# 68 late slots instead of 64, the second half's x in PSUM, and the low-part products last in each chunk

## What is computed

```python
def peer(x, w_query, sub_keys_1, sub_keys_2, expert_down, expert_up):
    ...                       # product keys: eidx [T, 128] expert numbers, g [T, 128] softmax weights
    def chunk(args):
        xi, ei, gi = args
        u = expert_down[ei]
        a = jax.nn.gelu(jnp.einsum('cd,ced->ce', xi, u)).astype(jnp.float32)
        w = (a * gi).astype(xi.dtype)
        return jnp.einsum('ce,ced->cd', w, expert_up[ei])
    ...
x = x + peer(rms_norm(x, norm_ffn_gain[l]), ...)
return rms_norm(x, norm_final_gain)
```

## Time and profile before

| | us |
|---|---|
| median of 3 runs | 2063.03 (2059.24 to 2063.68) |
| the profiled execution | 2062.69 |
| its span in the trace | 2060.8 |
| TensorE busy | 1896.1 (92% of the span) |
| VectorE busy | 1538.8 (75%) |
| ScalarE busy | 846.6 (41%) |
| POOL busy | 798.5 (39%) |
| data moved | 620.14 MB, mean 301 GB/s |

### The profile page before, as it was taken

The page is one execution under the profiler, slowest core; times in us unless marked ns, Lnnn a source line. Parts: engine busy times, 40 slices in busy tenths (PEclk is TensorE's granted clock), DMA queues, the critical chain, the costliest instruction groups (busy, mean ns, idle before and its releaser), DMA issues.

```text
span 2060.8 us, 28583 instructions
## 1 busy us (share of the span) xinstructions
PE 1896.1 (92%) x11587; PEld 1671.0 (81%) x11587; DVE 1538.8 (75%) x1856; ACT 846.6 (41%) x1108; POOL 798.5 (39%) x494
## 2 busy tenths in 40 slices
PE   8999999999999999788987466699999999999997
PEld 7989987999998789678887355578888888888876
DVE  5444446444465469899999999866888888999998
ACT  4333336333333443223322488344344444433433
POOL 1310300000000022755665788023454444777873
PEclk9999999999999999899999688799999999999999
DMA  7864540555566535999999999568999999999996
GB/s 253 294 212 164 168 139 22 165 182 183 184 224 229 191 133 210 398 426 420 425 421 413 362 427 427 212 228 326 384 407 399 392 385 383 378 408 400 395 397 268
DMA packets 142669, 620.14 MB, mean 301 GB/s; under 512 B 9680, under 2 KB 20192, under 8 KB 84464
## 3 DMA queue, kind: packets, MB, share of 16 engines
q0 software_dynamic: 46352, 336.11, 40.0%
q1 hardware_dynamic: 93712, 280.05, 37.5%
q10 hardware_dynamic: 2512, 2.75, 0.4%
HBM read 616.77 MB, written 2.10 MB: 300 GB/s over the span
## 4 chain that ended last, share of the span: by engine, by line
PE 72%; DVE 12%; POOL 7%; issue 5%; DMA 3%; ACT 1%; DVEq 0%; SPq 0%; ACTq 0%; POOLq 0%
PE psum L638 70%; POOL down_rows L1209 6%; DVE down_rows L2090 4%; DMA down_rows<-in_peer_expert_down_dram,eidx 2%; DVE w_lo L1748 1%; POOL pe_rows L1209 1%; ACT w_hi L1307 0%; PE psum L656 0%; DMA x_in<-in_x_dram 0%; DVE u_lo L2197 0%; DVE xres L2210 0%; DVE onehot L2050 0%; DVE onehot L2053 0%; DVE key L2055 0%; PE psum L981 0%
## 5 line engine op out<-in xcount | busy, mean ns | idle before, releaser
L1748 DVE TENSOR_TENSOR w_lo<-raw,w_hi 128x2048 fp32r<-128x2048 f32 x124 | 291.4, 2350 | 349.3 <-ACT w_hi L1307 349.2
L1307 ACT CAST w_hi<-raw 128x2048 fp32r<-128x2048 f32 x124 | 236.1, 1904 | 415.6 <-PE psum L638 415.6
L638 PE MATMUL psum<-u_hi,c_hi 128*128 128x512 f32 x1024 | 401.4, 392 | 3.9 <-POOL c_lo L1243 3.5
L638 PE MATMUL psum<-u_lo,c_hi 128*128 128x512 f32 x1024 | 399.4, 390 | 0.0
L638 PE MATMUL psum<-u_hi,c_lo 128*128 128x512 f32 x1024 | 399.4, 390 | 0.0
L2197 DVE TENSOR_TENSOR u_lo<-u_raw,u_hi 128x2048 fp32r<-128x2048 f32 x128 | 308.1, 2407 | 90.2 <-ACT u_hi L1657 89.0
L2090 DVE CUSTOM_DVE_ANT_0 down_rows<-down_rows,xn 128x2048 f32<-128x2048 f32 x157 | 354.1, 2286 | 6.2 <-DMA down_rows<-in_peer_expert_down_dram,eidx 4.6
L1209 POOL DMA_INDIRECT down_rows<-in_peer_expert_down_dram,eidx x157 | 271.8, 1732 | 129.2 <-issue 45.3
L638 PE MATMUL psum<-act_hi,w_hi 128*128 128x256 f32 x1088 | 310.5, 285 | 4.4 <-DVE w_lo L1748 4.4
L638 PE MATMUL psum<-act_hi,w_lo 128*128 128x256 f32 x1088 | 308.9, 284 | 0.0
L638 PE MATMUL psum<-act_lo,w_hi 128*128 128x256 f32 x1088 | 308.9, 284 | 0.0
(11 more groups left out here) (312 smaller groups left out, 3109.0 us busy)
## 6 DMA issues: line engine op xcount, KB each, us to landing
u_raw<-in_peer_expert_up_dram SPq DMA_DIRECT2D x128, 1024.0 KB, 6.6
raw<-in_w_in_dram SPq DMA_DIRECT2D x76, 1024.0 KB, 5.0
raw<-in_w_out_dram SPq DMA_DIRECT2D x16, 1024.0 KB, 5.0
raw<-in_peer_w_query_dram SPq DMA_DIRECT2D x16, 1024.0 KB, 5.0
raw<-in_w_up_nsa_dram SPq DMA_DIRECT2D x8, 1024.0 KB, 4.9
raw<-in_w_up_fox_dram SPq DMA_DIRECT2D x8, 1024.0 KB, 4.9
cmp_w<-in_k_cmp_w_dram SPq DMA_DIRECT2D x4, 1024.0 KB, 10.7
cmp_w<-in_v_cmp_w_dram SPq DMA_DIRECT2D x4, 1024.0 KB, 10.6
```

The source lines that it names most:

```text
L638: return nc.tensor.matmul(*a, skip_group_check=True, **k)
L1307: nc.scalar.copy(w_hi[:, p % 2], raw[:, p]).then_inc(hi_done, 1)
L1748: tt(w_lo[:, p % 2], raw[:, p], f32(w_hi[:, p % 2]), ALU.subtract).then_inc(lo_done, 1)
```

## The change

Four slots of the second half move from the gather stage to the late slots (`DENSE` 60, `LATE` 68), and the loops over slots run to `NT` = 188. The second half's x is put into banks 0 to 3 by four matmuls with the identity, as is already done for the first half (at `XRES_AT`), so `xres[:, 1]` is free from the first chunk on and serves as a sixth late buffer; the additions go to a tile of its own, `late_sum`, from step 67 on. In `up_chunk` the eight products with `u_lo` come last, behind a wait of their own, and a new semaphore `u_hi_used` tells ScalarE that the `u_hi` products before them are done. ScalarE does `u_high` ahead of `c_high`.

```diff
-LATE_H = 4
-DENSE = (SLOTS, LATE_H * TOPK)
+DENSE = (SLOTS, 60)
 LATE = SLOTS - DENSE[1]
-NG = (DENSE[0] + DENSE[1]) // GS
+NT = DENSE[0] + DENSE[1]
+NG = -(-NT // GS)
@@
-LATE_AT = (10, 74, 18, 82, 0)
-LATE_FREE = (16, 16, 32, 32, 0)
-LATE_EARLY = (1, 3, 5, 7, 9, 11, 13, 15)
+LATE_AT = (10, 74, 18, 82, 0, 146)
+LATE_FREE = (16, 16, 32, 32, 0, 0)
+LATE_EARLY = tuple(range(1, 17))
+LATE_SUM_FREE = 48
 LATE_C0 = 17
-LATE_A = 32
+LATE_A = 34
@@
-LATE_ADD = 71
+LATE_ADD = 67
@@ tensor
-            pe.wait_ge(W_out, NB + NB1)
-            pe.wait_ge(wT_done, 2)
-
-            def up_chunk(i, q, first=False, end=False):
-
-                pe.wait_ge(u_lo_done, i + 1)
+            for c in range(4):
+                pe.wait_ge(W_out, NB + NB1 - 1 + c // 2)
+                last = mm(psum[:, c, :], ident, xres[:, 1, 512 * c:512 * c + 512], start=True, stop=False)
+            last.then_inc(xres_in, 1)
+
+            def up_chunk(i, q, end=False):
+
+                pe.wait_ge(u_hi_done, i + 1)
                 pe.wait_ge(c_lo_done, i + 1)
                 for half in range(HALVES):
-                    hi, lo = c_hi[:, q % 2, 1 - half, :], c_lo[q % 2][:, 1 - half, :]
                     for c in range(4):
                         o, n = psum[:, 4 * (1 - half) + c, :], slice(512 * c, 512 * c + 512)
-                        mm(o, hi, u_hi[:, q % 2, n], start=first and half == 1, stop=False)
-                        mm(o, hi, u_lo[q][:, n], start=False, stop=False)
-                        last = mm(o, lo, u_hi[:, q % 2, n], start=False, stop=end)
+                        mm(o, c_hi[:, q % 2, 1 - half, :], u_hi[:, q % 2, n], start=False, stop=False)
+                        last = mm(o, c_lo[q % 2][:, 1 - half, :], u_hi[:, q % 2, n], start=False, stop=False)
+                last.then_inc(u_hi_used, 1)
+                pe.wait_ge(u_lo_done, i + 1)
+                for half in range(HALVES):
+                    for c in range(4):
+                        o, n = psum[:, 4 * (1 - half) + c, :], slice(512 * c, 512 * c + 512)
+                        last = mm(o, c_hi[:, q % 2, 1 - half, :], u_lo[q][:, n], start=False, stop=end)
                     last.then_inc(half_summed if half == 0 else chunk_used, 1)
@@ gpsimd, late_gather and the loop
                 elif LATE_FREE[r] == 0:
-                    pool.wait_ge(W_ps, NB + NB1)
+                    pool.wait_ge(xres_in, 2)
...
-            late_gather(0)
-            issued = 1
+            issued = 0
@@ scalar
                 if i >= 2:
-                    act.wait_ge(chunk_used, i - 1)
+                    act.wait_ge(u_hi_used, i - 1)
+                    act.wait_ge(u_lo_done, i - 1)
                 nc.scalar.copy(u_hi[:, i % 2, :], u_raw[i % 4][:]).then_inc(u_hi_done, 1)
...
             for i in range(2, NKEYS):
+                u_high(i)
                 c_high(i)
-                u_high(i)
@@ vector, late_add
-                ins = stt(xres[:, 1, cs], late_rows[r][:, cs], w, xres[:, 1, cs], ALU.mult, ALU.add)
+                if j == LATE - PRE:
+                    dve.wait_ge(c_lo_done, LATE_SUM_FREE)
+                    ins = ts(late_sum[:, cs], late_rows[r][:, cs], w, None, ALU.mult)
+                else:
+                    ins = stt(late_sum[:, cs], late_rows[r][:, cs], w, late_sum[:, cs], ALU.mult, ALU.add)
```

More of the change, by code:

```diff
@@ L503, in last_unit @@
             return hs if hs < FOX_H else FOX_H + 2 * (hs - FOX_H) + 1
-        ring_slots = [t for t in range(NG * GS) if t not in PE_SLOTS]
+        ring_slots = [t for t in range(NT) if t not in PE_SLOTS]
         def ring_at(t):
-            return ring_slots.index(t) if t < NG * GS else len(ring_slots) + t - NG * GS
+            return ring_slots.index(t) if t < NT else len(ring_slots) + t - NT
         down_slot, down_turn, down_before = [], [], []
@@ L1210, in gather @@
                     ap=eidx[:, half, slot:slot + 1], axis=0)).then_inc(landed, 16)
-            for t in range(NG * GS + PRE):
+            for t in range(NT + PRE):
                 half, slot = t // SLOTS, t % SLOTS
@@ L1582, in gelu_tanh_of @@
                 act.wait_ge(inner_done, half + 1)
-                hs = slice(0, DENSE[half] // TOPK)
-                A(pabf[:, 1, hs], pabf[:, 0, hs], ACT.Tanh, scale=GELU_C0).then_inc(tanh_done, 1)
+                inner, tanh = (pabf[:, l].rearrange("p h s -> p (h s)")[:, 0:DENSE[half]] for l in range(2))
+                A(tanh, inner, ACT.Tanh, scale=GELU_C0).then_inc(tanh_done, 1)
             def late_tanh(turn):
@@ L2168, in weights @@
                     pre_dot(0)
[L2169 removed]
+                g = gw[half].rearrange("p h s -> p (h s)")[:, 0:DENSE[half]]
+                gelu_outer(half + 1, a, g, w_pairs[:, 0:DENSE[1]] if half else g, g1, g2, w_done)
             def one_hots_0(b):
@@ L2252, in final @@
                 dve.wait_ge(row_loaded, 16)
-                x2 = psum[:, 4:8, :].rearrange("p k n -> p (k n)") if half == 0 else xres[:, 1, :]
+                x2 = psum[:, 4:8, :].rearrange("p k n -> p (k n)") if half == 0 else late_sum[:]
                 for cs in OUT_COLS:
@@ L2283, in _ @@
                     t = GS * G + q
-                    if t not in PE_SLOTS:
+                    if t not in PE_SLOTS and t < NT:
                         dot(t)
```

30 lines of the change are left out of this document (16 added, 14 removed).

## The result

The changed kernel takes 2071.83 us (median of 5 runs, 2067.13 to 2074.39), beside 2062.60 for the kernel before (now a median of 5 runs too): ratio 1.0045 [1.0033, 1.0058], **slower by 9 us**, where 16 us faster was forecast. Its profiled execution took 2069.88 us, with a span of 2068.1: 7.3 us above the span of before.

What follows compares the result with a forecast made beforehand. DMA engines were taken to bound the gather stage and TensorE the dense stage, with 5.6 us lost among the additions. 9.8 + 1.7 + 4.6 = 16.1 us won, 2062.69 to 2046.6 us; forecast 2042 to 2050, eight in ten 2041 to 2055.

Steps and rivals of the forecast that it cites:

- Four gathers and dots fewer: Gather stage: four 1 MB gathers saved at the DMA engines' pace of 2.46 us each, 9.8 us won.
- rival 2: End of the gather stage held by something else, half of the 9.8 us lost: 2051.5 us; chance 7%.
- The identity matmuls: Before chunk 0: four added matmuls hidden in TensorE's 2.6 us idle, costing nothing; 1.8 us without that cover.
- Two gathers ahead of the second `c_low`: Before chunk 1: gathers delaying `c_low` cost between nothing and 2.6 us; taken as nothing.
- The clock of chunk 0: Chunk 0: TensorE no longer idles before it, so its matmuls run at the higher clock, 1.7 us won.
- Low parts last: Among the additions: slack for `u_lo` grows to nearly 6 us; 5.6 us less 1.0 for late loads, 4.6 won.
- rival 1: Among the additions: `c_lo` or a late load replaces `u_lo` as the stall, 5.6 us stay: 2051.2 us; chance 14%.
- The end: After the last chunks: additions keep 3 us of slack and the first half's square ends before `residual`; nothing lost.
- Eight dots more beside steps 1 to 16: Early dense steps: extra dots hidden in VectorE's idle time, two buffers with 10.9 us each; without cover 8 x 2.3 us.
- The part on `c_low`: Under the new product order: late loads delay `c_high` and POOL, with two gathers in a row in seven steps; 1.0 us allowed.
- Rival 3: Among the additions: POOL becomes the bound with stretched `c_lo` and gathers, up to 2100 us; chance 7%.
- Rival 4: Dense stage: TensorE loses pace by the new order of banks, 31 us if one matmul in twenty slows: 2078; chance 2%.

Runs made afterwards that it cites:

- e1_order_alone: The kernel before with only the new order (products with `u_lo` last, `u_hi_used`, `u_high` ahead of `c_high`), 64 late slots: 2060.1 us, ratio 0.9992.
- e1_no_order: The changed kernel with the old order of products, the old wait and `c_high` ahead of `u_high`: 2068.8 us, ratio 1.0025.
- e3_halfp: The changed kernel with 14 of its 16 early gathers bringing rows of 64 tokens instead of 128: 2065.5 us, ratio 1.0016.
- e1_cap2: The changed kernel with at most two late gathers behind one `c_low`: 2062.8 us, ratio 1.0004.
- e3_14chi: The changed kernel without dots in steps 6 and 11, additions from step 69, one or two gathers per `c_low`, `c_high` first: 2046.4 us, ratio 0.9926.
- e3_12chi: As e3_14chi, but 12 of the first 16 steps with a dot (none in 4, 8, 12), additions from step 71: 2054.1 us, ratio 0.9962.

## Why the prediction was wrong

Point by point, in the prediction's own steps, from the profiled executions.

- *Four gathers and dots fewer*: predicted 9.8 us, measured 10.4 at `weights(1)` and 9.9 at chunk 0. Right, though the nearness is in part luck: the traces with 64 and with 68 late slots are 8.5 us apart in the mean, 2.1 us a slot instead of 2.46. The end of the gather stage was held by nothing else (rival 2 did not come).
- *The identity matmuls*: predicted nothing, measured some 0.5 us, which is what chunk 0 has gained less than `weights(1)`. `c_lo` was ready at 1335.77, but TensorE was still at the eight records of the identity matmuls (1333.27 on, 592 ns each, 0.43 us apart as in the earlier trace rows) and began chunk 0 at 1336.40. They were to be half as long at the higher clock. That misread: the granted clock was 1.00 there, and it is 1.00 here (POOL in the changed kernel; the window of the earlier trace rows in the kernel before; that of the changed kernel's eight records).

```profile
1335.04 0.73 POOL L1252 TENSOR_TENSOR c_lo<-W,c_hi 128x256 fp32r<-128x256 f32 x1 [54.34 <-ACT c_hi L1681]
```

```profile
1240.00:1243.60 3.60, 3.60 (x10) 1.66 (x9) 3.60 (x3) 3.54 (x10) 2.99 (x3) 1.00 1.01 426
```

```profile
1333.20:1336.90 3.70, 3.70 (x13) 1.72 (x10) 0.29 (x2) 3.49 (x5) 0.73 (x1) 1.00 0.00 0
```

- *Two gathers ahead of the second `c_low`*: predicted nothing; chunks 1 to 4 are 5.44 us apart. Right.
- *The clock of chunk 0*: predicted 1.7; chunk 0 took 5.89 us instead of 7.17, so 1.3.
- *Low parts last*: predicted 4.6 won. From chunk 33 on 5.8 us were lost before and 2.4 after, 3.4 won. The mechanism is right, as the lost times of e1_order_alone and e1_no_order show; the cost of `c_high` behind a late load was put at 1.0 us and was some 2. The waits of the additions for `u_lo` are gone; rival 1 came at one chunk only, 124, where a late load made `c_lo` late.
- *The end*: nothing, and it is nothing. From the last matmul to the end of the span it is 10.7 us in both.
- ***Eight dots more beside steps 1 to 16. "Two buffers alternate, each with 10.9 us for a gather and a dot. Hidden"***: this is the step that failed. It compared the work with the room, and did not add up the turn: gather, landing, dot, hand-over. The numbers were there. The landing of a load of the same size in the earlier trace rows, at a DMA share of 1.01, has a median of 8.6 us; with a dot of 2.3 that makes 10.9, no slack at all, and the traffic of these steps (2 MB in 5.44 us, 385 GB/s of the 427 seen) is near that load. Instead I took the idle time of VectorE for the criterion, an average that says nothing of a ring with a latency. It cost 9.2 us of the 13.5. The other 4.4 fall at chunks 15 and 16, where three gathers stand in a row. There the two causes are not separated: e3_halfp, whose turn closes, still loses 4.6 with the three in a row, but e1_cap2, whose turn does not, loses 4.2 with two.
- **The runs of gathers**: two buffers come free at the same chunk, and with one buffer more in use (`LATE_AT`) the gathers in a row in front of one `c_low` become four instead of three. The part on `c_low` counted gathers per step and "two gathers in a row in seven steps", and the step with four was not looked for, though the order of POOL's instructions shows it. At 2.2 + 0.3 us each, four gathers and a stretched `c_low` are 13 us, in front of a chunk that is due in 5.44. It cost 8.3 us at chunk 32, of which 1.8 are the lower clock behind the standstill. e1_cap2 took 7 of them back.
- *Rival 3*, POOL becomes the bound by stretched gathers, was put among the additions, where it did not come: chunks 33 to 119 lose nothing. Its mechanism did act, in the early steps, as 1.8 us of each turn.
- *Rival 4*, the order of banks: 5.44 us a chunk in either order; it did not come.

The sum over: 9.9 + 1.3 + 3.4 won, 21.9 lost in chunks 1 to 32: 7.3 us slower, the difference of the spans. Without these 21.9 us the changed kernel would have 2049.9 us, within the forecast. That e3_14chi, which takes both losses away, has the predicted 2046 is in part luck: it also gains about 2 us at the end by `c_high` first, which was not the change, and that stands in for what the order and the identity matmuls gave less than predicted.

What stays open: whether 16 dots would fit if each gather's issue were short. By the parts they would (9.7 less 1.8 of landing, 2.3 of dot and 0.3 of hand-over are 10.5 us of 10.9), but no run brought the gathers of all 16 back into the gap. Open too is what of the 4.4 us at chunks 15 and 16 belongs to the run and what to the ring. Nor is it shown why the early loss of e3_12chi and of e1_cap2 falls at chunk 4 already.
